# Tiles 4 and 5 of an MLP's widening as a pair of seven block products

## The reference, cut to what matters

```python
x = x + merged @ w_out
h2 = rms_norm(x, g_mlp)
x = x + jnp.square(jax.nn.relu(h2 @ w_up)) @ w_down    # 1024 -> 4096 -> 1024
```

## Time and profile before

| | us |
|---|---|
| median of 3 runs | 929.46 (929.38 to 929.7) |
| the profiled execution | 929.17 |
| its span, first to last instruction | 927.5 |
| TensorE busy | 912.6 (98%) |
| VectorE busy | 603.9 (65%) |
| ScalarE busy | 442.1 (48%) |

### The profile page before, as it was taken

One profiled execution on the slowest core, in us unless ns is written; L12 is line 12 of the kernel. 1 busy time (PEld: TensorE's weight loads), 2 busy tenths in 40 slices (PEclk: granted clock), 3 DMA queues, 4 the chain that ended last, 5 costly groups with the idle time before them and its releaser, 6 DMA issues.

```text
span 927.5 us, 17663 instructions
## 1 busy us (share of the span) xinstructions
PE 912.6 (98%) x7414; PEld 886.1 (96%) x7414; DVE 603.9 (65%) x815; ACT 442.1 (48%) x663; POOL 87.3 (9%) x142
## 2 busy tenths in 40 slices
PE   6999999999999999999999999999999999999998
PEld 5999999999999889999999999999999999999998
DVE  6589699511777746475568666666676666778453
ACT  7546323223876544444356544444444444446532
POOL 5190032201001210100000000000000000000000
PEclk9999999999999999999999999999999999999999
DMA  9531554824523576522323222322323223242203
GB/s 234 126 87 44 149 166 105 192 74 154 131 71 96 197 277 213 170 70 69 92 69 92 90 84 83 89 90 91 91 75 92 87 90 92 91 137 71 69 5 99
DMA packets 134694, 102.19 MB, mean 110 GB/s; under 512 B 18560, under 2 KB 124408, under 8 KB 134584
## 3 DMA queue, kind: packets, MB, share of 16 engines
q1 hardware_dynamic: 129096, 83.38, 30.7%
q0 software_dynamic: 5424, 17.65, 6.0%
q10 hardware_dynamic: 96, 0.04, 0.0%
HBM read 88.71 MB, written 12.21 MB: 109 GB/s over the span
## 4 chain that ended last, share of the span: by engine, by line
PE 92%; DVE 3%; ACT 2%; issue 1%; DMA 0%; ACTq 0%; DVEq 0%
PE dense L2278 65%; PE banks L2278 20%; PE scoreA L2278 3%; PE banks L2434 2%; PE dense L2434 1%; PE scoreB L2278 1%; DVE Llo L1735 1%; ACT t L1616 1%; DVE t L2102 1%; ACT whi L1323 1%; DVE Ssum L1711 0%; DMA xtok<-in_x_sample 0%; DVE wlo L1735 0%; DVE sm L2160 0%; ACT yh L1662 0%
## 5 line engine op out<-in xcount | busy, mean ns | idle before, releaser
L1735 DVE TENSOR_TENSOR wlo<-wraw,whi 128x1024 fp32r<-128x1024 f32 (+1 forms) x139 | 152.6, 1102 | 104.2 <-ACT whi L1323 91.9
L2278 PE MATMUL dense<-hid,whi 128*128 128x256 f32 (+1 forms) x1024 | 176.6, 294 | 0.1
L2278 PE MATMUL dense<-act_hi,whi 128*128 128x256 f32 (+1 forms) x736 | 168.1, 298 | 1.4 <-issue 1.4
L2278 PE MATMUL dense<-act_hi,wlo 128*128 128x256 f32 (+1 forms) x736 | 164.6, 294 | 0.3 <-DVE wlo L1735 0.3
L2278 PE MATMUL dense<-act_lo,whi 128*128 128x256 f32 (+1 forms) x736 | 164.4, 294 | 0.0
L2278 PEld LDWEIGHTS dense<-hid,whi 128*128 128x128 f32 x1024 | 152.5, 188 | 0.5 <-issue 0.4
L1323 ACT CAST whi<-wraw 128x1024 fp32r<-128x1024 f32 x100 | 110.1, 1103 | 45.6 <-PE banks L2278 44.1
L2278 PEld LDWEIGHTS dense<-act_hi,whi 128*128 128x128 f32 x736 | 123.9, 188 | 4.8 <-issue 4.1
L2278 PEld LDWEIGHTS dense<-act_hi,wlo 128*128 128x128 f32 x736 | 124.6, 188 | 0.5 <-DVE wlo L1735 0.5
L2278 PEld LDWEIGHTS dense<-act_lo,whi 128*128 128x128 f32 x736 | 124.7, 188 | 0.0
L2278 PE MATMUL dense<-hid,wlo 128*128 128x256 f32 (+1 forms) x512 | 108.8, 294 | 0.0
(11 more groups left out here) (366 smaller groups left out, 1571.2 us busy)
## 6 DMA issues: line engine op xcount, KB each, us to landing
wraw<-in_w_in SPq DMA_DIRECT2D x32, 512.0 KB, 4.9
wraw<-in_w_up SPq DMA_DIRECT2D x32, 512.0 KB, 4.0
wraw<-in_w_down SPq DMA_DIRECT2D x32, 512.0 KB, 3.6
gates_spill<-gst POOLq DMA_DIRECT2D x16, 288.0 KB, 3.1
page<-in_cache_k SPq DMA_DIRECT2D x16, 256.0 KB, 7.9
page<-in_cache_v SPq DMA_DIRECT2D x16, 256.0 KB, 7.5
wraw<-in_w_out SPq DMA_DIRECT2D x8, 512.0 KB, 3.8
wraw<-in_w_ple_gate SPq DMA_DIRECT2D x8, 512.0 KB, 3.6
```

The costliest lines, as they stand in the source:

```text
L1735: return nc.vector.tensor_tensor(out=lo, in0=whole, in1=f32(hi), op=ALU.subtract)
L2278: return nc.tensor.matmul(out, lhsT, rhs, start=start, stop=stop, skip_group_check=True)
```

## The change

`FIRSTPAIR` goes from 6 to 4: tiles 4 and 5 become a pair. The new order is up 0 to 3, down 0, down 2, pair 4, down 4, pair 6, down 6, pair 8, down 8, down 10, and from there as before. Down 0 follows up 3 at once; TensorE does k 0 to 2 of both its halves first (`hpart`) and then k 3 of each. `flush()` stands right behind up 3 and the events `xpair` 3, `xsplit` 2, `rscale` 2, `xsplit` 3 and `rscale` 3 stand together between the `hpart`s and the halves. `pair(1)` is followed by one down unit, `pair(2)` by two. `NPAIR` goes from 13 to 14 with it.

```diff
@@ units_of
     for f in range(8):
-        for i in range(0, 4, 2):
-            m, d = 4 * (f + 1) + i, [("down", 8 * f + 2 * n, 4, 2) for n in (i, i + 1)]
-            if m < FIRSTPAIR:
-                us += [("up", m, 8, 1), d[0], ("up", m + 1, 8, 1), d[1]]
-            else:
-                us += ([("pair", m, 8, 1), ("pair2", m + 1, 8, 1)] if f < 7 else []) + d
+        downs = [("down", 8 * f + 2 * n, 4, 2) for n in range(4)]
+        wide = [[("pair", m, 8, 1), ("pair2", m + 1, 8, 1)] if m < 32 else [] for m in (4 * f + 4, 4 * f + 6)]
+        if f == 0:
+            us += downs[0:2] + wide[0] + downs[2:3] + wide[1] + downs[3:4]
+        else:
+            us += wide[0] + downs[0:2] + wide[1] + downs[2:4]
@@
-FIRSTPAIR = 6
+FIRSTPAIR = 4
@@ schedule_of
-    def pair():
+    def pair(downs):
@@
         n[0] += 2
-        for j in range(2):
+        for j in range(2 * downs):
             half_unit()
-            event("hidlow", m + j)
-        for j in range(2):
-            half_unit()
+            if j < 2:
+                event("hidlow", m + j)
@@
     event("xpair", 2)
     event("xsplit", 1)
     unit()
+    flush()
+    for j in range(2):
+        event("hpart", n[0], j, 0, 3)
     event("xpair", 3)
     event("xsplit", 2)
     event("rscale", 2)
-    unit()
     event("xsplit", 3)
     event("rscale", 3)
     half_unit(split_first=False)
-    flush()
-    half_unit()
+    half_unit(split_first=False)
     event("rscale", 6)
     event("rscale", 7)
-    unit(2)
+    unit()
     for m in range(FIRSTPAIR, 32, 2):
         if m == LASTHID - 8:
             event("inv")
-        pair()
+        pair(2 if m >= 8 else 1)
```

## The result

The changed kernel takes 935.47 us (median of 4 runs, 934.61 to 935.83) against 929.42 for the kernel before on the same chips: ratio 1.0065, 95% interval 1.0053 to 1.0078. It is slower by 6.1 us. The forecast was 936.0, slower.

The account below looks back on a forecast made before the run. TensorE's matmuls were taken to bound the MLP; -1.53 -0.07 +6.13 (idle) +2.0 (slow restart) = +6.5 on the profiled 929.17 gives 935.7, or 936.0 as median, 0.7% slower; range 933.0 to 938.0.

Parts of the forecast that it names:

- What bounds the kernel: In the MLP, every microsecond of TensorE matmuls sets the end, while VectorE and ScalarE keep their distance.
- The saving: Tiles 4 and 5 as a pair of seven products instead of two units take 1.53 us off TensorE.
- The further 0.07 of the sum: Delay of up tile 5 at its PSUM slot in the old order, counted as a further gain of 0.07 us.
- The first cover: Hidden tile 3, needed for down unit 0's last k, is in time by 1.7 us; cost nothing.
- The second cover: Down unit 2 waits for its slot until VectorE adds down unit 0's first half; TensorE idles 6.13 us.
- The low bound of this term: Idle before down unit 2 is 3.4 us if the two blocks and the xu wait cost VectorE nothing.
- The clock: After the idle, TensorE restarts at the lower clock level, costing 2.0 us more.
- The first rival: TensorE stalls before down unit 2 but the clock stays up: 934.0 us, chance 0.24.
- The bounds, 1.3 to 2.6: Range in us for the slow restart's loss after the idle, from 3.6 to 5.2 us of slow stretch.
- The closer pairs: Pairs with one down unit between them: block preparation and bank reads stay in time, cost nothing.
- The rival of a second stall: Pair 6 waits for first blocks or pair 8 for the bank, 1 to 3 us twice: 937.5 to 941, chance 0.06.
- The rival on the other side: VectorE adds down unit 0's first half by 499.0, so no stall: 927.9 us, chance 0.06.

Follow-up runs that it names:

- fifth experiment: Changed kernel, same work reordered: token sums earlier, blocks 0 and 1 between down unit 0's halves, fewer k begun early; 928.16 us, ratio 0.9989.
- seventh kernels: Order of the fifth experiment, but tiles 4 and 5 as two ordinary units behind down unit 2 instead of a pair; 929.78 us, ratio 1.0008.
- second experiment: Changed kernel with rscale 6 and 7 moved ahead of the two halves of down unit 0, no work added; 937.42 us, ratio 1.0091.
- the third: Changed kernel without the flush() behind up 3, so blocks 0 and 1 of pair 4 come behind down unit 0's adds; 934.21 us, ratio 1.0052.
- sixth experiment: Changed kernel with only xpair 3 left ahead of down unit 0's halves; xsplit 2, rscale 2, xsplit 3, rscale 3 follow; 930.35 us, ratio 1.0013.
- first experiment: Changed kernel with 42 filler matmuls into an unread PSUM bank, inside the idle stretch before down unit 2; 933.82 us, ratio 1.0053.
- fourth experiment: Changed kernel with down unit 0's halves ahead of xpair 3 through rscale 3, and rscale 6 and 7 behind pair 4; 928.92 us, ratio 0.9998.

## Why the prediction was right, point by point

- *What bounds the kernel*: right. TensorE's stretches around the change add up to +6.07, and the medians differ by 6.05: what TensorE does and waits for sets the time.
- *The saving*: worked out as 1.53. Pair 4 lasts 11.10 us, which makes 1.54; the fifth and seventh kernels differ by 1.62, their traces by 1.54. The further 0.07 of the sum was counted twice: rows 3 give up 5 its 6.32 us with that delay in it.
- *The first cover* (36 of 48 matmuls hide hidden tile 3): right, there is no wait at k 3. The fifth experiment shows how thin it is: with 30 matmuls ahead, and other work ahead of the tile on VectorE, 0.34 us of wait came up, 0.6 in starts.
- *The second cover*: the step that carries the result. 6.13 us worked out, 6.12 measured. The chain was right in each step: with 0.52 taken off, the add starts at 504.39, where the prediction had 504.39. And `xpair` 3 does wait for `xu` behind the cast of block 1, as ScalarE's rows show (0.52 late like the others; the prediction had `xu` at 497.07):

```profile
497.06 0.62 ACT L1339 CAST whi<-wsum 128x512 fp32r<-128x512 f32 x1 [0.91 <-DVE wsum L1711]
497.59 1.44 ACT L1489 ACTIVATE xu<-R,gains 128x576 f32<-128x576 f32 x2
```

The second experiment added 1.54 us to the chain and 1.59 came out, the third and sixth took parts of it away.
- *The low bound of this term* (3.4 us) was for blocks and the wait for `xu` both at nothing. With the blocks gone 4.07 were left by starts, as a wait for `xu` of 0.58 stays.
- *The clock*: the direction was right, the size a little high: 2.0 taken, 1.49 in the profile, 1.3 to 1.4 by the first experiment. That is most of the 0.5 us by which 936.0 missed. The argument was a reading of the start as the lower level in spite of the printed 1.00. No run settles what the start ran at; what the trace bears out is that a slow restart follows an idle stretch in the middle of a run, with 0.57 granted. The first rival (clock stays up, 934.0) is what the first experiment makes, at 933.82. The rule of the Trainium skill ("TensorE: Matmul & The Clock Gate", "HAM oscillation — how this bites in real kernels") held, and the trace agrees, with 0.57 for 3.59 us. The bounds, 1.3 to 2.6, hold 1.49 here, 1.72 in the second kernel (8.04 for 6.32) and 1.63 in the sixth, and miss the third's 2.63 by a hair. That this kernel's price lay within 0.5 of the 2.0 is in part luck: nothing in the working tells 1.5 from 2.6, and both came.
- *The closer pairs*: no wait, 23.75 us from down unit 4 to down unit 6 with VectorE busy 17.02 of them. The rival of a second stall is out for this order. The fourth experiment shows where it lives: not in the cadence, but in a pair that starts with VectorE behind.
- *The rival on the other side* (the add in time, 927.9): its point of decision was right. Orders in which the add comes at 499 were run, and they give 928.92 and 928.16. They needed other places for some 6 us of VectorE's work, which the change leaves ahead of the add, and with them came smaller waits that kept the time above 927.9.

## What to carry to other kernels

When a matrix engine is nearly always busy, a change that saves matmuls also takes away cover: list who reads each accumulator slot that changes neighbours, and add up what stands ahead of that reader on its own engine, operation by operation. Here 1.5 us of saved matmuls uncovered 6.1 us of elementwise work that was just hidden before, with no margin at the slot. And what such a wait costs is not its length alone: each hole of 2 us or more that was traced here was followed by slow matmuls, so cutting a hole from 6.1 to 4.1 us brought only 0.9 us, while closing it brought 6.2 us (the fourth experiment) and 7.1 (the fifth).

## What the runs showed of the hardware beyond that

- The clock fell to the lower level in or just behind holes that are, by starts, 7.7, 6.1, 4.1 and 2.0 us long, in the one traced execution of each; the slow matmuls behind them had 0.53, 0.57, 0.51 and 0.57 granted. The slow part cost 1.7, 1.5, 2.6 and 1.6 us. Its price does not follow the length of the hole: in the first two the clock was already down in part of the hole (granted 0.79 and 0.70 over it), in the third less of it (0.85), in the last not at all (1.00). Times and mean clocks of the third and the sixth experiment say that it differs from one execution to the next as well.
- 42 matmuls of no use in the hole, at 288 columns each, kept the granted clock at 1.00 and made the kernel 1.3 us faster than the idle hole did (each against the kernel before on its own chip).
- In the first microseconds the records print 1.00 while 16 transposes last 0.42 us each, for 0.27 in the later ones. In the slow stretch behind the hole, where the records do show 0.57, matmuls are drawn out by about as much (0.68 for 0.42, two at a time). So the printed clock of a trace's start may be wrong, and durations are the safer guide; no run shows what slowed the start.
